# Attention heads of an MLA layer run as one loop over score blocks, with the low parts of P, K and Q on GpSimd

## The reference

```
q = (c_q @ w_q_b)                        # 768 -> 8 x 96 (64 nope, 32 rope)
kv = (c_kv @ w_kv_b)                     # 256 -> 8 x (64 + 64)
k_nope, v = kv[..., :64], kv[..., 64:]
k = concatenate([k_nope, k_pe])          # k_pe is one for all heads
q, k = rmsnorm_2(q, g_qn), rmsnorm_2(k, g_kn)
q, k = rope on the last 32 of each
s = q @ k.T / sqrt(96), causal
o = softmax(s) @ v
```

## Time and profile before

| | |
|---|---|
| median of the runs | 3545.39 us |
| span of the profiled execution | 3557.2 us |
| busy: TensorE, VectorE, ScalarE, GpSimd | 3139.6, 1569.9, 711.5, 833.7 us |
| mean granted TensorE clock | 0.929 |

### The profile page before, as it was taken

One profiled execution on the slowest core, in us unless ns is written; L12 is line 12 of the kernel. 1 busy time (PEld: TensorE's weight loads), 2 busy tenths in 40 slices (PEclk: granted clock), 3 DMA queues, 4 the chain that ended last, 5 costly groups with the idle time before them and its releaser, 6 DMA issues.

```text
span 3557.2 us, 40295 instructions
## 1 busy us (share of the span) xinstructions
PE 3139.6 (88%) x16640; PEld 2803.0 (79%) x16640; DVE 1569.9 (44%) x1540; ACT 711.5 (20%) x1191; POOL 833.7 (23%) x646
## 2 busy tenths in 40 slices
PE   6975676999999995999997888898999997888899
PEld 4754565777777774999997787798999997877789
DVE  4677456333333336500115665663520114655671
ACT  2132310000000002000112454400000111544410
POOL 2321012233333331333322000022333332000012
PEclk9987789999999997999998888899999998988899
DMA  2100011111111111112112000042112112000131
GB/s 98 47 30 27 0 71 38 47 46 43 47 47 41 47 47 66 54 42 96 48 42 77 8 13 13 31 152 94 42 48 90 48 42 84 13 13 7 37 145 71
DMA packets 46201, 182.47 MB, mean 51 GB/s; under 512 B 5744, under 2 KB 5872, under 8 KB 45552
## 3 DMA queue, kind: packets, MB, share of 16 engines
q1 hardware_dynamic: 31248, 113.19, 10.0%
q10 hardware_dynamic: 14816, 67.28, 4.9%
HBM read 150.06 MB, written 30.39 MB: 51 GB/s over the span
## 4 chain that ended last, share of the span: by engine, by line
PE 70%; DVE 20%; ACT 4%; issue 3%; DMA 1%; POOL 1%; DVEq 0%; ACTq 0%; SPq 0%; POOLq 0%
PE acc L353 61%; PE aux L648 2%; DVE act_lo L1214 2%; DVE ff_split L1214 2%; DVE small L1665 2%; DVE ff_split L1213 1%; DVE residual L1279 1%; PE acc L629 1%; PE acc L613 1%; DVE act_hi L1213 1%; DVE work L1230 1%; DMA spill_g<-work 1%; DVE work L1223 1%; ACT pool_split L1146 1%; PE aux L686 1%
## 5 line engine op out<-in xcount | busy, mean ns | idle before, releaser
L353 PE MATMUL acc<-act_hi,w_hi 128*128 128x348 f32 (+1 forms) x3488 | 868.4, 351 | 106.0 <-DVE act_lo L1214 39.2
L353 PE MATMUL acc<-act_lo,w_hi 128*128 128x348 f32 (+1 forms) x3488 | 855.7, 347 | 0.0
L353 PE MATMUL acc<-act_hi,w_lo 128*128 128x348 f32 (+1 forms) x3488 | 853.0, 346 | 0.0
L353 PEld LDWEIGHTS acc<-act_hi,w_hi 128*128 128x128 f32 x3488 | 619.3, 193 | 168.1 <-issue 70.5
L321 POOL TENSOR_TENSOR small<-shape_consts 128x1 f32<-128x1 f32 x212 | 47.1, 222 | 2666.4 <-PE acc L353 2666.4
L353 PEld LDWEIGHTS acc<-act_lo,w_hi 128*128 128x128 f32 x3488 | 624.4, 193 | 44.0
L353 PEld LDWEIGHTS acc<-act_hi,w_lo 128*128 128x128 f32 x3488 | 620.8, 192 | 42.1
L324 POOL TENSOR_TENSOR w_lo<-w_raw,w_hi 128x1024 fp32r<-128x1024 f32 x212 | 568.1, 2680 | 17.0
L353 PE MATMUL acc<-ff_split,w_hi 128*128 128x512 f32 (+1 forms) x1408 | 356.6, 379 | 22.0 <-DVE ff_split L1214 22.0
L1431 DVE TENSOR_TENSOR residual<-acc,residual 128x1024 f32<-128x1024 f32 (+1 forms) x88 | 108.1, 1229 | 468.2 <-PE acc L353 468.2
L353 PEld LDWEIGHTS acc<-ff_split,w_hi 128*128 128x128 f32 x1408 | 257.6, 190 | 71.1 <-DVE ff_split L1214 26.5
(11 more groups left out here) (215 smaller groups left out, 2887.3 us busy)
## 6 DMA issues: line engine op xcount, KB each, us to landing
w_raw<-in_wstream SPq DMA_DIRECT2D x215, 512.0 KB, 3.5
spill_x<-residual ACTq DMA_DIRECT2D x2, 4176.0 KB, 12.7
spill_m<-residual ACTq DMA_DIRECT2D x2, 4176.0 KB, 13.2
spill_g<-work ACTq DMA_DIRECT2D x2, 4176.0 KB, 14.3
residual<-spill_m ACTq DMA_DIRECT2D x16, 522.0 KB, 5.9
work<-spill_g ACTq DMA_DIRECT2D x16, 522.0 KB, 7.9
residual<-spill_x ACTq DMA_DIRECT2D x16, 522.0 KB, 4.3
residual<-in_xT ACTq DMA_DIRECT2D x8, 512.0 KB, 9.9
```

The source lines that it names most:

```text
L353: ins = nc.tensor.matmul(acc[0:m, s, p, 0:w], wt[:, ws, w0 + j * m:w0 + j * m + m], x[:, k, p * w:p * w + w], start=(first and t == 0), st ...
```

## The change

The attention stage becomes one loop on each engine: for h from -1 to 7, for n from 0 to 14. In step n TensorE computes score block n of head h, a part of head g = h + 1's projection and value product n - 2. Everything of the projection, the norms, the turned values and the rough scores goes by the three token pieces (QP = 384 columns). PSUM is assigned anew: one bank each for q, k/v, norm sums and turned values (acc_q, acc_k, acc_n), two for score blocks (acc_s), one for rough scores and turned maxima (acc_r); aux stays for the value products. A rough score of more than 512 columns gets one maximum for each 512, and the parts are joined by a minimum of the negated values. Value buffers become two (even and odd heads), the ring of P has four places instead of five, and each has its own float32 copy. The low parts of P, K and Q move from VectorE to GpSimd; GpSimd's loop over weight units is cut in ranges, and within the heads the split of one unit follows low part 2.

In the cut below, low_keys and low_queries are like low_values, for a piece of K and Q after k_hi and q_hi; query_sum is like key_sum, after q_squared, and its bank is freed by qn_free; turn_values waits for the bank too and is freed by v_lo. The Ln in key_scale and query_scale raises kn_free and qn_free. scores waits for p_hi of block n - 2, weigh_values for p_lo of its block.

```diff
+        acc_q, acc_k, acc_n = (acc[:, 0, i, :] for i in range(3))
+        acc_s, acc_r = (acc[:, 1, 0, :], acc[:, 1, 1, :]), acc[:, 1, 2, :]
...
         def _(pool):
+            def low_values(l, h, n):
+                k = block_no(l, h, n)
+                pool.wait_ge(sems["p_hi"], k)
+                nc.gpsimd.tensor_tensor(prob(k, 1)[:, 0:w], prob32(k)[:, 0:w], prob(k, 0)[:, 0:w].bitcast(F32),
+                                        ALU.subtract).then_inc(sems["p_lo"], 1)
...
+                for h in range(-1, MH):
+                    g = h + 1
+                    for n in range(NB):
+                        if h >= 0:
+                            low_values(l, h, n)
+                            if n == 2:
+                                split(heads + 2 + h, (heads + h) % 2, 16 * ((heads + 2 + h) // 2 + 1))
+                        if g < MH:
+                            if n in (5, 9, 13):
+                                low_keys(l, g, n // 4 - 1)
+                            if n in (6, 10, 14):
+                                low_queries(l, g, (n - 6) // 4)
...
         def _(pe):
+                def key_sum(g, pc):
+                    if n_free[0] is not None:
+                        pe.wait_ge(*n_free[0])
+                    pe.wait_ge(sems["k_squared"], k)
+                    nc.tensor.matmul(acc_n[:, 0:w], ones96, X[:, 6, c0:c0 + w], start=True,
+                                     stop=True).then_inc(sems["k_sum"], 1)
+                    n_free[0] = (sems["kn_free"], k)
...
+                def rough_scores(h, i, p):
+                    if r_free[0] is not None:
+                        pe.wait_ge(*r_free[0])
...
+                    r_free[0] = (sems["rough_max"], rough_no(l, h, i, p))
...
+                for h in range(-1, MH):
+                    g = h + 1
+                    more = g < MH
+                    for n in range(NB):
+                        if h >= 0:
+                            scores(h, n)
+                            if n == 0:
+                                turn_maxima(h, 1)
+                            if n in (1, 2, 3):
+                                rough_scores(h, 5 + n, 0)
+                            if n == 4:
+                                rough_scores(h, 8, 2)
+                            if n == 5:
+                                turn_maxima(h, 2)
+                        if more:
+                            if n in (8, 9, 10):
+                                rough_scores(g, n - 8, 0)
+                            if n == 11:
+                                turn_maxima(g, 0)
+                            if n in (12, 13, 14):
+                                rough_scores(g, n - 9, 0)
+                            if n in (0, 4, 8):
+                                key_value_part(g, n // 4)
+                            elif n < 12:
+                                query_part(g, n // 4, n % 4 - 1)
+                            if n in (3, 7, 11):
+                                key_sum(g, n // 4)
+                            if n in (4, 8, 12):
+                                query_sum(g, n // 4 - 1)
+                            if n in (6, 10, 13):
+                                turn_values(g, (n - 6) // 3)
+                            if n in (13, 14):
+                                rough_scores(g, n - 9, 1)
+                        if h >= 0 and n in (1, 2, 3):
+                            rough_scores(h, 5 + n, 1)
+                        if h >= 0 and n >= 2:
+                            weigh_values(h, n - 2)
+                        if h >= 1 and n < 2:
+                            weigh_values(h - 1, NB - 2 + n)
...
         def _(act):
+                        if h >= 0:
+                            exponents(h, n)
+                            if n == 0:
+                                maximum_row(h, 1)
+                            if n == 2 and h >= 1:
+                                inverse_sums(h - 1, 2)
+                            if n == 4:
+                                inverse_sums(h, 0)
+                            if n == 5:
+                                maximum_row(h, 2)
+                            if n == 9:
+                                inverse_sums(h, 1)
...
+                        if more:
+                            if n == 11:
+                                maximum_row(g, 0)
+                            if n in (4, 8, 12):
+                                key_scale(g, n // 4 - 1)
+                            if n in (0, 4, 8):
+                                key_value_evict(g, n // 4)
+                            if n in (5, 9, 13):
+                                query_scale(g, n // 4 - 1)
+                            if n in (7, 11, 14):
+                                high_values(g, (n - 7) // 3)
+                            if n in (3, 7, 11):
+                                query_squares(g, n // 4)
...
         def _(dve):
                 dve.wait_ge(sems["g_spilled"], 16 * (l + 1))
+                for h in range(2):
+                    v1, v2 = values(h, 0), values(h, 1)
+                    do(vec.tensor_copy(v1[:, 0:8, 64:128], ones[:, 0:64].unsqueeze(1).to_broadcast([P, 8, 64])))
...
+                            if n == 3 and h >= 1:
+                                head_out(h - 1, 2)
+                            if n in (1, 2, 3):
+                                maximum(h, 5 + n, 0)
+                                maximum(h, 5 + n, 1)
+                            if n == 4:
+                                maximum(h, 8, 2)
+                                maxima_of(2)
+                            if n == 5:
+                                head_out(h, 0)
+                            if n == 10:
+                                head_out(h, 1)
...
+                        if more:
+                            if n in (4, 8, 12):
+                                query_table(g, n // 4 - 1)
+                            if n in (5, 9, 13):
+                                key_norm(g, n // 4 - 1)
+                            if n in (6, 10, 14):
+                                query_norm(g, (n - 6) // 4)
+                            if n in (7, 11):
+                                low_part_values(g, (n - 7) // 4)
+                            if n in (8, 9, 10):
+                                maximum(g, n - 8, 0)
+                            if n in (12, 13, 14):
+                                maximum(g, n - 9, 0)
+                            if n in (13, 14):
+                                maximum(g, n - 9, 1)
+                            if n == 14:
+                                maxima_of(1)
+                                low_part_values(g, 2)
```

More of the change, by code:

```diff
@@ new lines, in query_part @@
+                def query_part(g, pc, part):
+                    k = wave(l, g, pc)
+                    c0, w = QP * pc, piece_width(pc)
+                    if part == 0 and k > 1:
+                        pe.wait_ge(sems["q_free"], k - 1)
+                    for j in (2 * part, 2 * part + 1):
+                        if g == 0 and pc == 0:
+                            pe.wait_ge(sems["a_ready"], a_count + j + 3)
+                        for t, (wt, x) in enumerate(((Wh, Ah), (Wh, Al), (Wl, Ah))):
+                            ins = nc.tensor.matmul(acc_q[:, 0:w], wt[:, w_head[0], j * P:j * P + P],
+                                                   x[:, j, c0:c0 + w], start=(j == 0 and t == 0),
+                                                   stop=(j == 5 and t == 2))
+                    if part == 2:
+                        ins.then_inc(sems["q_raw"] if pc < NQP - 1 else sems["unit_done"], 1)
@@ new lines, in query_sum, with turn_values @@
+                def query_sum(g, pc):
+                    k = wave(l, g, pc)
+                    w = piece_width(pc)
+                    pe.wait_ge(*n_free[0])
+                    pe.wait_ge(sems["q_squared"], k)
+                    nc.tensor.matmul(acc_n[:, 0:w], ones96, qsq[k % 2][:, 0:w], start=True,
+                                     stop=True).then_inc(sems["q_sum"], 1)
+                    n_free[0] = (sems["qn_free"], k)
+                def turn_values(g, pc):
+                    k = wave(l, g, pc)
+                    pe.wait_ge(*n_free[0])
+                    pe.wait_ge(sems["k_free"], k)
+                    for i in range(3):
+                        c0 = min(P * (3 * pc + i), LASTQ)
+                        ins = nc.tensor.transpose(acc_n[:, 64 * i:64 * i + 64], R[64:128, 16, c0:c0 + P],
+                                                  ident[64:128, 64:128])
+                    ins.then_inc(sems["v_turned"], 1)
+                    n_free[0] = (sems["v_lo"], k)
@@ new lines, in turn_maxima @@
+                def turn_maxima(h, pc):
+                    pe.wait_ge(*r_free[0])
+                    if pc:
+                        pe.wait_ge(sems["max_ready"], 2 * (l * MH + h) + pc)
+                    for i in range(3 * pc, 3 * pc + 3):
```

(30 more changed lines are left out.)

617 lines of the change are left out of this document (292 added, 325 removed).

## The result

The changed kernel takes 3561.13 us (median, 3559.55 to 3569.37), the kernel before 3545.5 beside it: ratio 1.0055 [1.004, 1.0069], slower. The forecast was 3483, with 3410 to 3550 as its range. It was wrong in sign and in size. The loss itself is small beside what the kernel before does from one execution to the next: with 11 to 23 runs in each later set it took 3532 to 3563 us (medians 3546.1 to 3548.0), at a mean clock of 0.940 in the shortest and 0.929 in the longest. So the change lost some 13 to 16 us by the medians, and what is certain is that it gained nothing.

A forecast was written before the change was run, and what follows sets the result against it. It took TensorE as the bound, with idle time and low clock. Per head 36.9 work + 7.3 waits + 0.8 hand-offs + 1.5 clock = 46.5 us; with the stage ends, 62 us saved: 3483 us, range 3410 to 3550.

The forecast's parts named there:

- The clock, 1.5: Slots 11 to 14: clock falls in part of the heads, costing only in slots 0 and 1, 1.5 us a head.
- rival C: Two low-clock stretches a head remain, at slots 4 to 7 and 11 to 14: period 51, 3546 us; chance 0.10.
- TensorE's work, 36.9: TensorE's products per head at full clock, priced per matmul, with cutting into pieces taken as free: 36.9 us.
- The waits, 7.3: TensorE's waits for single banks in slots 4, 7, 8 and 11 to 14: 7.3 us a head.
- hand-offs, 0.8: Uncovered hand-offs between engines: about 0.1 us each, 0.8 together per head.
- A: Short gaps keep the clock full and hide one another better: period 42.5 us, 3427 us; chance 0.15.
- D: Single banks serialise, with 19 us of uncovered waits a head: period 57 us, 3630 us; chance 0.11.
- About 44 at full clock: Old kernel's steady head: 51.2 us less two low-clock stretches of about 3.5 to 3.8 each is near 44.
- The other engines: Per head: ScalarE 27 us, VectorE 24 plus 7 waiting on GpSimd's memory use, GpSimd 22; all below TensorE's work.
- The start of the stage: First score block of the attention stage in layer 1 at 1941, 14.6 us after the old mark.
- The last head, 23.5: Last head, without projection: 18.5 us of products, 3 for maxima, 2 for the last value products: 23.5 us.
- signs of being wrong: Period over 51; acc_n waits every third slot; slow casts; value products waiting for GpSimd's low parts; no slot 11 idle.

The follow-up runs named there:

- the second experiment: The changed kernel with unread TensorE products (fillers) only in the waits of slots 11 to 14, none in slot 4: 3520.92 us, ratio 0.9934.
- the first experiment: The changed kernel with unread TensorE products (fillers) in the waits of slots 4 and 11 to 14, no wait removed: 3520.55 us, ratio 0.9933.
- the fastest kernel: The changed kernel with reordered lists, later spill wait, and 18 and 2 unread products before the rough scores of slots 13 and 14: 3472.86 us, ratio 0.9787.

## Why the prediction was wrong

Its sum for a head was 36.9 work + 7.3 waits + 0.8 hand-offs + 1.5 clock = 46.5. Measured: 39.8 + 6.8 + 0.8 + 3.8 = 51.2. The first three terms are those of heads at full clock (47.4 with fillers, 47.3 in the one without), the last is what is left to 51.2. Two terms failed, the clock by 2.3 and TensorE's work by 2.9, and neither alone makes up the miss of 4.7. By its own steps:

1. *The clock, 1.5: mis-sized by 2.3.* I said that half speed costs only where it runs into slots 0 and 1, "between 0 and 3.8, I take 1.5", and that it would fall in part of the heads. It fell twice, for about 10 us together, in eight of the twelve steady heads. Slot by slot against the head at full clock, slot 11 took 6.3 instead of 5.5, slot 12 2.9 instead of 2.7, slot 14 3.4 instead of 2.9 and slot 0 5.2 instead of 3.0 (score block, turned maxima and key part, from 2144.29 to 2149.50). So the larger part, 2.2, did run into slot 0, but 1.6 came in slots 11 to 14, where I had put the cost at nothing.

   This is the mechanism of rival C (51 us a head, 3546 us), which I gave 0.10. Its two places were given as slots 4 to 7 and 11 to 14, and both fell in 11 to 0. Its period of 51 is partly luck: it took the same 36.9 of work and 6 us for the two stretches, which cost 3.8, so that two errors of opposite sign met.

   The part of the page that I cited beside it (the Trainium skill, "TensorE: Matmul & The Clock Gate", "A second HAM failure mode: psum-queue depth-cycling") says of another kernel, in bf16, that micro-idles between groups of matmuls make the clock swing between its two levels. The trace agrees in kind: the waits of slots 11 to 14 are 0.85 to 1.75 us, and with fillers in them every steady head but the first of a layer ran at full clock. It does not follow that every short wait matters: 1.35 in slot 4, with work around it, did nothing (the second experiment), and the one head with all the waits and a full clock says that they do not suffice.

2. *TensorE's work, 36.9: mis-sized by 2.9.* At full clock, with waits and fillers taken off, the fifteen slots of the first experiment take 3.0, 3.15, 2.8, 3.5, 3.1, 2.9, 3.0, 2.9, 2.9, 1.8, 2.3, 3.1, 1.6, 1.8, 1.8, before rounding 39.8. The mean miss is 0.2 a slot. In the head without fillers, from each group's start to the next one's and with the waits off, the projection takes 12.9 (I had 11.3), the value products 8.9 (7.3) and the rough scores 4.4 (3.7), while the two sums take 2.7 (3.6). I had priced products from the inside of long groups, and each slot has five to eight short groups; that the changes between groups are the cost is my reading, and no run varied them alone. "Cutting is free" was wrong: by the same count the old head's own work is 38.1.

3. *The waits, 7.3, and hand-offs, 0.8: right.* At full clock 1.35, 0.41, 0.26, 2.18, 0.86, 0.89, 0.85 against 1.35, 0.6, 0.4, 1.7, 1.1, 1.1, 1.1, which is 6.8. What the unfilled head has beside them over the filled one is 0.16 at each of five waits: 0.8 for the hand-offs. Rivals A and D fall here: A's 42.5 is below what the head takes even at full clock, and D's 19 us of waits are 7.6.

4. *"About 44 at full clock" for the old head: wrong.* It is 46.3 with fillers and at least 45.1 without. It is no term of the sum, but it was the room for the gain that I saw. It came from two low stretches at 3.5 to 3.8 us each, some 7.2; they cost 4.9 to 6.1. At full clock the new head takes 47.3 and the old one at most 46.3, a loss.

5. *The other engines: right.* ScalarE 28.2 against 27, GpSimd 21.7 against 22. VectorE 26.2 against 24 with 7 lock waits on top: the waits are mostly not there. GpSimd's subtract was estimated at 1.0, 0.8 and 0.55 us; in the trace it is 1.01, 0.77 and 0.54, here in one pair that ran side by side with VectorE and in the last head:

```profile
1921.60 1.46 DVE L1804 SCALAR_TENSOR_TENSOR residual<-residual,params 128x384 f32<-128x384 f32 x1
1921.64 1.01 POOL L388 TENSOR_TENSOR ff_split<-residual,ff_split 128x384 fp32r<-128x384 f32 x1 [26.79 <-DVE ff_split L1816]
```
```profile
2325.38 0.77 POOL L379 TENSOR_TENSOR pool_split<-work,pool_split 128x276 fp32r<-128x276 f32 x1 [0.34 <-ACT pool_split L1292]
2326.43 0.54 POOL L379 TENSOR_TENSOR pool_split<-work,pool_split 128x168 fp32r<-128x168 f32 x1 [0.27 <-ACT pool_split L1292]
```

The collision exists: VectorE's operation takes 0.79 at its shortest in layer 1 and 1.46 here, and ends 0.41 after GpSimd's. But each delay is below 1 us, VectorE's casts of 384 columns keep to 0.36, and VectorE has 25 us of slack a head. The section "SBUF: two separate sides" of the Trainium skill's "SBUF — State Buffer" calls it a lock; the pair above agrees that one waits for the other, and VectorE's 26.2 us of busy time shows that it does not decide here.

6. *The start of the stage: right.* First score block predicted at 1941, measured 1940.9.

7. *The last head, 23.5: too small by 6.3.* It took 29.8. It starts at low clock, and waits 0.85, 0.85 and 1.53 for maxima, as much as I had put down for them. With no projection between them the value products wait for GpSimd's low parts, which I had costed at nothing: 1.6 us in four waits. This and a period over 51 are two of the signs of being wrong that I had named. Two of the waits are:

```profile
2319.59 0.61 PE L815 MATMUL aux<-pool_split 128*128 128x276 f32 x3 [0.49 <-POOL pool_split L379]
...
2322.43 0.65 PE L815 MATMUL aux<-pool_split 128*128 128x276 f32 x3 [0.70 <-POOL pool_split L379]
```

GpSimd needs 1.01 for 384 columns and 0.77 for 276, and a block without projection gives it little more.

In the kernel with all fillers, which has none in the last head, that head runs at full clock and takes 27.6. So 2.2 of the 6.3 were clock and 4.1 the rest: GpSimd's low parts and TensorE's own work.

The sum, then: 7 heads x 4.5 + 6.3 = 38 us in layer 1, by which 363.6 becomes 401.3. In a head of 51.2 the 4.7 are 2.9 of work and 2.3 of clock, less 0.5 by which the waits were taken too large. What stays open is what sets where, and whether, the clock falls in a head: a change in slot 13 alone moved it, and two neighbouring heads of one kernel with the same waits differ in it.

## What to carry to other kernels

Before a structure is changed for its idle time, fill the idle time with unread products and run that: here it gained more than any order of the lists without it (53 us in the old kernel, 41 in the new), it shows what the engine's own work and waits cost at full clock, and it is the base that the new structure has to beat. A wait of 1 to 2 us on TensorE can cost itself and then half speed for the next 3 to 10 us, so look where that time falls: 2.2 of the 3.8 us came in slot 0, which has no wait, and in the pass where TensorE waits for VectorE anyway it cost 1 to 2 us. Put the fillers into the wait itself, where idle time is left behind them: elsewhere they gave nothing, or cost time. Sum TensorE's work from whole slots of mixed groups and not from the inside of long ones.

## What the runs showed of the hardware

- One wait of 2.2 us was followed by some 10 us at 1.2 GHz in most heads of the kernel with reordered lists and the later spill wait; eighteen products of 128 columns in it and two in the next wait took that away, 42.4 us in the program.
- A full clock over a head did not need a head without waits: 1.8 us in four waits of at most 0.7 stand in the fastest kernel's at 1.00, and 6.8 us, with one wait of 1.75, in a head at 1.00 of the kernel with the later spill wait.
- The unchanged kernel took 3532 to 3563 us from run to run, with a mean clock of 0.940 in the shortest and 0.929 in the longest.
- Two quite different orders gave the same 51.2 us a head, and a third, with the low parts on VectorE, as well. Equal periods were no sign of an equal bound: at full clock the first two are at most 46.3 and 47.3.
